# Value projection of a differential-attention layer moved into the attention loop, one head at a time

## The reference

```python
xm, om, i_pre, f_pre, qd, kd, vd, g_a, g_b = split_columns(h @ w_in)
...
qd = partial_rope(qd.reshape(B, T, NH_D, 2, DH_D), pos)
kd = partial_rope(kd.reshape(B, T, NH_D, 2, DH_D), pos)
vd = vd.reshape(B, T, NH_D, DV_D)
...
s = jnp.einsum("bqhmd,bkhmd->bhmqk", q, k) * (DH_D ** -0.5)      # 8 heads, 2 maps each
s = jnp.where(k_pos[None, :] <= q_pos[:, None], s, -jnp.inf)
p = jax.nn.softmax(s, axis=-1)
a = p[:, :, 0] - lam * p[:, :, 1]
o = jnp.einsum("bhqk,bkhv->bqhv", a, v)
```

## Time and profile before

| | us |
|---|---|
| median of 3 runs | 1619.62 (1618.68 to 1620.36) |
| the profiled execution | 1618.32 |
| its span, first to last instruction | 1616.5 |
| PE, DVE, ACT busy | 1570.4, 1019.6, 686.8 |

### The profile page before, as it was taken

One profiled execution on the slowest core, in us unless ns is written; L12 is line 12 of the kernel. 1 busy time (PEld: TensorE's weight loads), 2 busy tenths in 40 slices (PEclk: granted clock), 3 DMA queues, 4 the chain that ended last, 5 costly groups with the idle time before them and its releaser, 6 DMA issues.

```text
span 1616.5 us, 29922 instructions
## 1 busy us (share of the span) xinstructions
PE 1570.4 (97%) x12266; PEld 1487.9 (92%) x12266; DVE 1019.6 (63%) x1675; ACT 686.8 (42%) x1125; POOL 4.5 (0%) x20
## 2 busy tenths in 40 slices
PE   8999999999999989999999999999998999999997
PEld 8899999999988668999999976679998999999997
DVE  5888888443782445643336689674458988886333
ACT  5555546222332434522211257572246555555222
POOL 0000000000000000000000000000000000000000
PEclk9999999999999999999999999999999999999999
DMA  6233333332322661233333250553322333323321
GB/s 151 79 105 105 87 97 94 95 86 67 82 78 57 236 218 48 77 87 85 105 93 94 76 193 27 191 175 91 91 79 79 105 105 105 105 79 108 90 78 68
DMA packets 246829, 164.64 MB, mean 102 GB/s; under 512 B 8350, under 2 KB 229779, under 8 KB 246714
## 3 DMA queue, kind: packets, MB, share of 16 engines
q1 hardware_dynamic: 246424, 162.46, 34.7%
q10 hardware_dynamic: 290, 0.57, 0.1%
HBM read 145.43 MB, written 16.42 MB: 100 GB/s over the span
## 4 chain that ended last, share of the span: by engine, by line
PE 85%; DVE 6%; ACT 4%; DMA 2%; issue 2%; SPq 1%; DVEq 0%; ACTq 0%
PE ps L461 41%; PE ps L985 25%; PE ps L941 3%; PE ps L1334 2%; PE ps L1298 1%; PE ps L1485 1%; PE ps L1128 1%; PE ps L1177 1%; PE ps L1610 1%; PE ps L1383 1%; PE ps L1540 1%; PE ps L444 1%; DVE small L3166 1%; PE ps L1654 1%; DMA Cb<-in_state_C 1%
## 5 line engine op out<-in xcount | busy, mean ns | idle before, releaser
L428 ACT ACTIVATE w_hi<-raw 128x1024 fp32r<-128x1024 f32 (+1 forms) x110 | 126.6, 1152 | 411.6 <-PE ps L461 395.3
L461 PE MATMUL ps<-xn_hi,w_hi 128*128 128x272 f32 (+1 forms) x848 | 245.7, 290 | 0.7 <-issue 0.7
L461 PE MATMUL ps<-xn_hi,w_lo 128*128 128x272 f32 (+1 forms) x848 | 246.1, 290 | 0.0
L461 PE MATMUL ps<-xn_lo,w_hi 128*128 128x272 f32 (+1 forms) x848 | 245.1, 289 | 0.0
L432 DVE TENSOR_TENSOR w_lo<-raw,w_hi 128x1024 fp32r<-128x1024 f32 (+1 forms) x110 | 147.3, 1340 | 154.7 <-ACT w_hi L428 154.5
L461 PE MATMUL ps<-h_hi,w_hi 128*128 128x280 f32 (+1 forms) x572 | 166.0, 290 | 0.0
L461 PE MATMUL ps<-h_hi,w_lo 128*128 128x280 f32 (+1 forms) x572 | 165.8, 290 | 0.0
L461 PE MATMUL ps<-h_lo,w_hi 128*128 128x280 f32 (+1 forms) x572 | 165.2, 289 | 0.0
L461 PEld LDWEIGHTS ps<-xn_hi,w_hi 128*128 128x128 f32 x848 | 159.9, 189 | 1.4 <-issue 1.3
L461 PEld LDWEIGHTS ps<-xn_hi,w_lo 128*128 128x128 f32 x848 | 159.8, 188 | 0.0
L461 PEld LDWEIGHTS ps<-xn_lo,w_hi 128*128 128x128 f32 x848 | 159.3, 188 | 0.0
(11 more groups left out here) (514 smaller groups left out, 3871.0 us busy)
## 6 DMA issues: line engine op xcount, KB each, us to landing
raw<-in_w_in SPq DMA_DIRECT2D x55, 512.0 KB, 3.7
rawg<-in_ffn_w_gate SPq DMA_DIRECT2D x44, 512.0 KB, 3.9
rawu<-in_ffn_w_up SPq DMA_DIRECT2D x44, 512.0 KB, 5.2
raw<-in_ffn_w_down SPq DMA_DIRECT2D x32, 704.0 KB, 4.7
Cb<-in_state_C SPq DMA_DIRECT2D x32, 256.0 KB, 3.8
out<-Cb SPq DMA_DIRECT2D x32, 256.0 KB, 2.9
pages<-in_cache_k SPq DMA_DIRECT2D x16, 512.0 KB, 4.2
pages<-in_cache_v SPq DMA_DIRECT2D x16, 512.0 KB, 4.7
```

The lines of the kernel that those rows point to most:

```text
L428: act.activation(w_hi[s][:, 0:p.nk, :], raw[s][:, 0:p.nk, :], ACT.Copy).then_inc(hi_done[s], 1)
L461: mm = pe.matmul(ps[:, bank + half, 0:p.half], w[s][:, k, :], x[:, i, cols], start=first and k == 0 and a == 0, stop=last and k == p.nk - ...
```

## The change

The projections are ordered keys, queries, values. `KROWS` puts the turning of key rows between the query tiles; ACT copies them into `vtok`, from where SP stores them, all before the values need that place. The stages "rotary" and "attend" end as stages of their own. Only the value tile of head 0 is projected ahead of attention. The tile of head h (1 to 7) is projected inside the loop at the step of (h, 0), behind its scores and `transposed`; two steps on its 560 tokens are turned (`v_rows`) and copied (`v_copy`). Its weights are split at step (h-1, 1). This takes banks 6 and 7, so turned probabilities have bank 4 alone and outputs bank 5 alone. The copies of queries for the samples (`sample_queries`) move to step 2 of attention. The page buffers are used in another order.

```diff
-        order = [up1, down1, p_xm, p_om, p_a, p_q, p_kv, p_b, p_wo, up2, down2]
+        order = [up1, down1, p_xm, p_om, p_a, p_k, p_q, p_v, p_b, p_wo, up2, down2]
...
+        KROWS = {2: (0, 1), 3: (2,), 4: (3,), 5: (4,), 6: (5,)}
...
-        SLOTS = [i % 5 for i in range(13)] + [3, 4, 0]
+        SLOTS = [3, 0, 1, 2, 4] * 3 + [3]
...
+        V_PARTS = {-1: (), 0: ((0, 0, DT), (1, 0, DT)), 1: ()}
+
+        def v_at(g):
+
+            return [(h, g - step(h, 0)) for h in range(1, HD) if -1 <= g - step(h, 0) <= 2]
+
+        def split_at(g):
+
+            return [h for h in range(2, HD) if g == step(h - 1, 1)]
...
+            for n in range(2 * DT):
+                p, t, _ = rotated(n)
+                load(sp, p, t // 2, t % 2)
+                if n >= 2:
+                    exchange(n - 2)
+                if n >= DT + 4:
+                    store_k(n - DT - 4)
...
+            def v_part(h, half, k0, k1):
+
+                if half == 0 and k0 == 0:
+                    pe.wait_ge(lo_done[h % 2], p_v.before + h // 2 + 1)
+                    if h >= 1:
+                        more(pe, vtok_ready, h)
...
+            def v_rows(h):
+
+                pe.wait_ge(evac[h % 2], p_v.ev0 + h // 2 + 1)
...
+            for t in range(DT):
+                pe.wait_ge(evac[t % 2], t // 2 + p_q.ev0)
+                product(pe, p_q, t // 2, t % 2, 2 * (t % 2), xn_hi, xn_lo)
+                for i in KROWS.get(t, ()):
+                    k_rows(i)
...
                     scores(g)
                 if 3 <= g < G + 3:
                     transposed(g - 3)
+                between(g)
                 if g >= 4:
                     output(g - 4)
...
             for g in range(G + 5):
+                if g >= 5:
+                    o_copy(g - 5)
                 if 3 <= g < G + 3:
                     at_copy(g - 3)
-                if g >= 5:
-                    o_copy(g - 5)
+                if g == 1:
+                    v_copy(0)
+                for h, n in v_at(g):
+                    if n == 2:
+                        v_copy(h)
...
                     e.then_inc(e_ready, 1)
+                for h in split_at(g):
+                    split_hi(act, p_v, h // 2, h % 2)
...
+            v.tensor_copy(own_k, qkv[:, DT:2 * DT, NP_:T]).then_inc(own_ready.sem, 1)
+            rope(2 * DT - 1)
+
+            def v_out(h):
+
+                v.wait_ge(mm_done[h % 2], p_v.before + h // 2 + 1)
+                if h >= 2:
+                    more(v, vt_full, h - 1)
+                v.tensor_tensor(tok(t2[h % 2]), two(6), tok(rn), ALU.mult).then_inc(evac[h % 2], 1)
+
+            v_out(0)
...
             for g, (h, i) in enumerate(ITEMS):
+                for h_, n in v_at(g):
+                    if n == 2:
+                        v_out(h_)
                 v.wait_ge(s_full, g + 1)
...
                 if g >= 1:
                     combine(g - 1)
+                if g == 2:
+                    sample_queries()
+                for h_ in split_at(g):
+                    split_lo(v, p_v, h_ // 2, h_ % 2)
```

More of the change, by code:

```diff
@@ L483, in loop @@
             body(n - 1, *((p.next, 0) if p.next is not None and not late(p.next) else (None, 0)))
-        STAGES = ["load", "project", "states", "heads", "om", "a_qkv", "rotary", "attend", "sample"]
+        STAGES = ["load", "project", "states", "heads", "om", "a_qkv", "sample"]
         def begin(eng, name):
@@ L574, in build @@
         st_n = sem("st_n")
-        st_k = [sem(f"st_k{i}") for i in range(2)]
+        st_k = sem("st_k")
         st_c = [sem(f"st_c{i}") for i in range(2)]
@@ new lines, in _, with store_v @@
+            for h in range(2):
+                load(sp, p_v, 0, h)
+                exchange(2 * DT - 2 + h)
+                store_k(4 + h)
+            for h in range(2, 4):
+                load(sp, p_v, h // 2, h % 2)
+            sp.wait_ge(in_vecs, 16 * 9)
+            def store_v(part):
+                h0, n_ = V_STORES[part]
+                more(sp, vtok_ready, h0 + n_)
+                for i, (t0, n) in enumerate(BLOCKS):
+                    dst = v_prompt[0, 0, t0:t0 + n] if i < 5 else v_sample[0].rearrange("b t h d -> (b t) h d")
+                    sp.dma_start(dst[:, h0:h0 + n_, :].rearrange("t h d -> t (h d)"),
+                                 vtok[0:n, i, 128 * h0:128 * (h0 + n_)]).then_inc(stored, 16)
@@ L902, in page @@
             def page(b, g):
                 return bass.ds(sp.value_load(page_sb[0:1, 2 * b + g:2 * b + g + 1], min_val=0, max_val=N_POOL - 1), 1)
+            for h in range(4, HD - 1):
+                load(sp, p_v, h // 2, h % 2)
             for i, (is_v, b) in enumerate(PAGES):
+                if i == 1:
+                    store_v(0)
+                    load(sp, p_v, HD // 2 - 1, 1)
+                    for s in range(2):
+                        sp.wait_ge(lo_done[s], p_v.before + p_v.n)
+                if i == 2:
+                    sp.wait_ge(mm_done[0], p_v.before + p_v.n)
+                if i == 3:
+                    store_v(1)
+                    sp.wait_ge(mm_done[1], p_v.before + p_v.n)
+                if i == 4:
+                    store_v(2)
@@ L1566, in _ @@
             pair(p_a, (xn, (hm_hi, hm_lo)), first=1)
[L1567 to L1578, removed]
@@ L1579, in _, with k_rows @@
-            end(pe, pe_stage)
-            more(pe, mask_ready, 2)
[L1584 to L1589, removed]
+            pair(p_k, (xn, xn))
+            def k_rows(i):
+                t0, nt = BLOCKS[i]
+                b = krows_bank(i)
+                if i == 0:
+                    pe.wait_ge(rot_ready, DT)
+                if i >= 2:
+                    ring_done(pe, kr(i - 2))
+                for f in range(DT):
+                    mm = transpose(ps[0:nt, b + f // 4, 128 * (f % 4):128 * (f % 4) + 128], qkv[:, DT + f, t0:t0 + nt], 128)
+                mm.then_inc(ring_full, 1)
@@ new lines, in _ @@
+            for t in range(DT):
[8 more added lines that the diff above has]
+                        more(pe, vtok_ready, h)
+                cols = slice(half * H2, half * H2 + H2)
+                for k in range(k0, k1):
+                    for a, (w, x) in enumerate(((w_hi, xn_hi), (w_hi, xn_lo), (w_lo, xn_hi))):
+                        mm = pe.matmul(ps[:, 6 + half, 0:H2], w[h % 2][:, k, :], x[:, k, cols],
+                                       start=k == 0 and a == 0, stop=k == DT - 1 and a == 2)
+                if half == 1 and k1 == DT:
+                    mm.then_inc(mm_done[h % 2], 1)
@@ new lines, in v_rows, with between @@
+            def v_rows(h):
+                pe.wait_ge(evac[h % 2], p_v.ev0 + h // 2 + 1)
+                for blk, (t0, nt) in enumerate(BLOCKS):
+                    c0 = 128 * (blk % 4)
+                    mm = transpose(ps[0:nt, 6 + blk // 4, c0:c0 + 128], t2[h % 2][:, t0:t0 + nt], 128)
+                mm.then_inc(vt_full.sem, 1)
+            def between(g):
+                if g == 1:
+                    v_rows(0)
+                for h, n in v_at(g):
+                    if n == 2:
+                        v_rows(h)
+                        continue
+                    for half, k0, k1 in V_PARTS[n]:
+                        v_part(h, half, k0, k1)
@@ L2292, in _ @@
             act.wait_ge(mm_done[1], p_a.before + p_a.n)
-            plain(p_q)
-            plain(p_kv)
-            end(act, act_stage)
+            plain(p_k)
+            for t in range(DT):
+                split_hi(act, *((p_q, t // 2 + 1) if t + 2 < DT else (p_v, 0)), t % 2)
+                for i in KROWS.get(t, ()):
+                    nt = BLOCKS[i][1]
+                    act.wait_ge(ring_full, kr(i) + 1)
+                    copy(vtok[0:nt, i, :], wide(krows_bank(i), nt, D)).then_inc(ring_act, 1)
             copy(ident_m[:, :], ident).then_inc(mask_ready.sem, 1)
```

185 lines of the change are left out of this document (91 added, 94 removed).

## The result

The changed kernel takes 1643.72 us (median of four runs, 1641.88 to 1650.21) against 1619.72 (1618.68 to 1620.36): a ratio of 1.0158, 95% interval 1.0141 to 1.0174. It is slower by 24.0 us. The profiled execution took 1642.89 us, 24.6 more than the one of before, with a span of 1641.1 us and a mean granted clock of 0.991 (before 0.996).

What follows compares the result with a forecast made beforehand. PE was taken as full in the projections and nearly full in attention. Key rows 5.3, joint 10.7, heads 1 to 6 104.9 and head 7 13.0 make 133.9 against 119.4 us: 14.5 more, 1634; range 1625 to 1643.

Steps and rivals of the forecast that it cites:

- Key rows: 48 turns of keys between query tiles, where PE is full: 5.3 us more, nothing hidden and nothing lost.
- The joint: From the end of value tile 0 to the scores of head 1, with DVE late: 10.7 us together.
- Heads 1 to 6: Each head with its value tile, PE waiting 2.57 us for `v_out` behind the split: 104.9 us for six.
- Head 7: Splits nothing behind itself, so `v_rows` waits 0.2 us; 13.0 us from its start to its last scores.
- The drain: After head 7's last scores, up to the sample stage: the sum ends at those scores, with no term for it.
- by my walk both copies end at least 0.5 us ahead: Single banks 4 and 5: copies finish before PE needs the bank; otherwise at most 0.6 us twice a head, 8 us.
- the clock stays 1.00: Expected sign in the new profile: granted clock at full level, so waits add nothing beyond their length.
- the fall of the clock as a rival: Tiles behind the waits run at half clock, 6.15 us more each, 37 for six: 1671 us; chance 0.03.
- the forecast: PE waits for `v_out` in six heads; 14.5 us slower, 1634, or 1627 to 1640; chance 0.73.
- the short chain: From block's end to `v_out`, overlap of 0.1 us at each of five hand-overs: 3 us less over six heads.

Runs made afterwards that it cites:

- experiment 3: In the changed kernel, PE computes 19 unread matmuls ahead of `v_rows` in heads 1 to 6, filling its wait; 1638.26 us, ratio 1.0120.
- experiment 1: In the changed kernel, the next head's weights are split one step earlier, at step (h-1, 0), for all heads but 1; 1626.57 us, ratio 1.0049.
- 5: On top of experiment 1, `sample_queries` moves from step 2 to step (1, 0), inside head 1's block; 1622.23 us, ratio 1.0021.
- 6: On top of experiment 1, the outputs of head 7 go to banks 6 and 7 in place of bank 5; 1624.72 us, ratio 1.0025.
- 7: Experiment 1 with the edits of 5 and 6, and the first row maximum ahead of `v_out(0)`; 1621.47 us, ratio 1.0008.
- 9: The kernel of experiment 7 with 19 unread matmuls ahead of `v_rows(0)` at the joint; 1620.88 us, ratio 1.0006.
- experiment 4: In the changed kernel, `split_lo`'s subtraction is done twice inside attention (heads 2 to 7), lengthening DVE's work ahead of `v_out`; 1656.05 us, ratio 1.0224.

## Why the prediction came out as it did

The direction and the mechanism held, and the largest term was sized well. The loss was forecast at 14.5 us and is 24.0. By the terms of its sum, in the profiled execution:

- **Key rows, "hidden and nothing lost", 5.3.** PE shows no idle time in the key and query tiles. Value tile 0 starts at 892.79, where 886.7 (936.0 less eight tiles of 6.16) and 5.3 give 892.0: 0.8 more. All of it arose ahead of the key tiles, which start 0.9 later than the old stage did; the key rows themselves cost 5.2.
- **The joint, 10.7.** Measured 12.0, from 899.0 to 911.01. The part behind the first maximum was right (8.5 against 8.3 forecast). The maximum came 3.6 us after value tile 0 and not 2.4, since the raw weights of head 1 were 1.2 us late. Rows of SP, ACT and DVE:

```profile
890.37 1.57 SPq L424 DMA_DIRECT2D raw<-in_w_in  x1
...
895.29 1.06 ACT L429 ACTIVATE w_hi<-raw 128x1024 fp32r<-128x1024 f32 x1 [5.78 <-DMA raw<-in_w_in]
...
902.54 0.41 DVE L3269 TENSOR_REDUCE small<-ps 128x2 f32<-128x256 f32 x1
```

  ACT idled 5.78 us for them. The load went out when the walk had it, behind an exchange of four transfers and a store on SP. The walk took a landing of 3.7 us from the median of before; here 4.9 us lie between the start of the issue and ACT's start, and the issue alone took 1.57, where most took under half a microsecond. What made it long I did not test. In the projections this is hidden, as was said; at the joint DVE works on the split and everything is queued behind it.
- **Heads 1 to 6, 104.9.** Measured 111.8 (911.01 to 1022.84). Undisturbed heads came out at 17.04, 17.02 and 18.55 against 16.86, 16.86 and 18.3; the waits at 2.40 in a head without a meta step against 2.57. Some 1.5 us of the 6.9 are such small differences. The other 5.5 are the clock. For heads 5 and 6 experiment 3 shows it: fill the wait, and they fall by 2.7 and 1.4 us while heads 2, 3 and 4 don't move. Head 1 has the same work as head 5 and took 19.72 us, 1.4 more than head 5 with the clock up (18.36); this third part is read from the lengths.
- **Head 7, 13.0.** From 1022.84 to 1036.1 it took 13.3, and `v_rows` waited for nothing.
- **The drain, carried over unchanged.** 9.5 against 7.9. Here "by my walk both copies end at least 0.5 us ahead" fails: I walked it inside a head, where a block of 6 us lies in between, and not at the end, where none does. The wait of 1.39 us and the half clock behind it replace two waits of 0.55 and 0.58 us, and the end comes 1.6 us later.

The differences sum to 0.8 + 1.3 + 6.9 + 0.3 + 1.6 = 10.9, which with 14.5 makes, but for rounding, the 25.3 us by which the stretch grew.

**The step that failed** is the premise of the sum that "the clock stays 1.00": the term for the clock was nothing, and it measured 5.5 us in the heads alone, with a part of the drain's 1.6 on top. No other difference is larger than 1.6. I weighed the fall of the clock as a rival with "the old trace shows no fall at any pause", and gave it 3%. That reading was wrong. The earlier trace rows can't show it: a digit stands for 40 us, and 9 for anything from 90% up. The old trace does show falls, only not in the stages I looked at: at PE's two longest waits, of 2.50 us (ending at 12.39) and 2.24 us (ending at 572.51). Two windows of the kernel before, outside every stage of the argument:

```profile
8.00:16.00 8.00, 5.26 (x38) 4.95 (x37) 3.20 (x6) 2.03 (x4) 0.00 (x0) 0.85 1.08 221
...
568.00:576.00 8.00, 5.76 (x50) 4.23 (x49) 3.18 (x6) 2.02 (x4) 0.00 (x0) 0.84 0.85 285
```

And I priced it as all or nothing, a whole tile at half clock in each of six heads, 37 us. The fall came in three of six heads, and cost 1.4 to 2.7 us each, since it was over before the next block began. With the price that the runs showed, the rival and the forecast are one case: 14.5 + 5.5. The range had a slip of its own: its low end of 1627 doesn't follow from the short chain, which takes 3 us from 1634.
The Trainium skill, "TensorE: Matmul & The Clock Gate" (Part 1), says that idle time brings the throttled clock back and that the same kernel can find a different number of slow matmuls from run to run. The runs agree on both: in the changed kernel's profile the falls stand at or behind idle times of 1.39 to 2.85 us, and its four runs have mean granted clocks from 0.986 to 0.991.

**Cause, as far as it is shown.** The delay of `v_rows` behind the split: shown, by taking it away in two ways (17 and 19 us) and by lengthening it (12 us more for 7.6 of added work). The clock's part: shown for heads 5 and 6 by the filler, read from lengths for head 1. Of the 7.5 us that experiment 1 still lost, 5.9 went with the edits of 5, 6 and 7 together; how they divide is less sure, since each alone moves the median by little more than the runs scatter. Why the gain didn't come with the waits gone: the change moves seven blocks of 6.15 us into heads that, as the prediction read them, had 0.3 us idle each; a tile costs PE the same anywhere, and experiments 7 and 9, with the waits in the heads gone, end level with the old kernel.

**Open.** Why a wait of 2.40 us brings a fall in head 6 and none in heads 2 and 3: the length alone doesn't decide it, and I have no experiment on what does. Why the clock falls in the sample stage of some profiles behind a wait of 0.98 us. Where the 0.9 us ahead of the key tiles arose. A block at another place in the head was not tried.

## What to carry to other kernels

When a block of matmuls is put in front of a short step, write down the other engine's queue from the block's end, not from the tile's: here the evacuation of a finished tile stood behind a split that nobody needed yet, and one line that swaps them, or that moves the split under the block, was worth 17 of 24 us. Before moving work "into idle time", sum that time at its place: where the engine is full in both orders, the best that a clean version can reach is a tie. And price each new pause of PE twice, its length and a possible spell at 1.2 GHz behind it; a filler that nobody reads tells the two apart. Look for such spells in windows of a few microseconds over the whole program, since a digit of the page that stands for 40 us hides them.

## What the runs showed of the hardware

- An idle time of TensorE of 1.4 to 2.9 us was enough, some of the time, for the granted clock to fall to 1.2 GHz at it or up to 1.6 us behind it; waits of 2.29 and 2.40 us in the same profile had no fall, and all six waits of 3.56 to 4.11 us in experiment 4's profile had one. In one window of 4 us the mean clock then lay between 0.50 and 0.65.
- Matmuls whose product is thrown away kept the clock up, at no cost where PE would have waited anyway: the kernel with 114 of them more is 5.5 us faster than without. They did not end every fall: one stood in head 1's block, behind a wait that was not filled.
- The changed kernel's four runs lie 8.3 us apart, the four with the pauses filled 1.4. That is no measure of the pauses by itself: 17 runs of the old kernel lie 10.5 us apart. The longest of the changed kernel's four, 1650.21 us, has the lowest mean clock, 0.986.
